# Attention stage of a fused encoder layer: four transpose slots instead of three, a chained minimum for the softmax, and the gate product moved to GpSimd

## The reference, cut to what matters

```python
logits = jnp.einsum('btgrd,btkgd->btgrk', qg, kg).astype(jnp.float32) * (A_HEAD_DIM ** -0.5)
dist = jnp.abs(q_pos[None, :, None] - sel).astype(jnp.float32)
logits = logits - slopes[None, None, :, :, None] * dist[:, :, None, None, :]
logits = jnp.where(valid[:, :, None, None, :], logits, -jnp.inf)
prob = jax.nn.softmax(logits, axis=-1).astype(v.dtype)
out = jnp.einsum('btgrk,btkgd->btgrd', prob, vg)
...
merged = (ga * ((o_a * jax.nn.silu(za)) @ w_a)
```

## Time and profile before

| | us |
|---|---|
| median of 3 runs | 3288.54 (3285.65 to 3290.68) |
| the profiled execution, its own time | 3291.84 |
| its span, first to last instruction | 3290.2 |
| PE busy in it | 2874.0 |
| DVE busy in it | 2378.2 |
| ACT busy in it | 1602.6 |
| POOL busy in it | 1268.2 |

### The profile page before, as it was taken

The page is one execution under the profiler, slowest core; times in us unless marked ns, Lnnn a source line. Parts: engine busy times, 40 slices in busy tenths (PEclk is TensorE's granted clock), DMA queues, the critical chain, the costliest instruction groups (busy, mean ns, idle before and its releaser), DMA issues.

```text
span 3290.2 us, 43028 instructions
## 1 busy us (share of the span) xinstructions
PE 2874.0 (87%) x14677; PEld 2576.1 (78%) x14677; DVE 2378.2 (72%) x4343; ACT 1602.6 (49%) x2638; POOL 1268.2 (39%) x875
## 2 busy tenths in 40 slices
PE   6999998999999989889551778888886999599998
PEld 6999998999999989889430555666666899488886
DVE  7478855839999999998437777787776555455564
ACT  4474787777776766764012555565562000211111
POOL 1100677777787858655222221111002332111120
PEclk9999999999999999999775999999998999799999
DMA  4434223333332323222663222112004555311220
GB/s 153 126 127 149 73 97 105 114 97 112 104 107 92 108 74 103 86 73 95 210 156 111 52 56 48 40 32 52 22 15 166 170 162 181 133 63 62 78 67 33
DMA packets 286182, 321.04 MB, mean 98 GB/s; under 512 B 37025, under 2 KB 258977, under 8 KB 282413
## 3 DMA queue, kind: packets, MB, share of 16 engines
q1 hardware_dynamic: 149037, 176.64, 18.1%
q10 hardware_dynamic: 135648, 137.80, 12.7%
q0 software_dynamic: 1312, 4.26, 0.4%
HBM read 194.46 MB, written 123.48 MB: 97 GB/s over the span
## 4 chain that ended last, share of the span: by engine, by line
PE 46%; DVE 36%; issue 6%; ACT 6%; DMA 4%; POOL 2%; ACTq 1%; SPq 0%; DVEq 0%; POOLq 0%
PE psum L1182 14%; PE psum L2064 12%; DVE s_high L427 10%; PE psum L1939 8%; DVE a_l L1770 4%; DVE a_ptlo L1789 3%; PE psum L1673 2%; PE psum L1709 2%; ACT s_ajunk L410 2%; DVE s_cand L429 2%; ACT v_product L820 1%; DVE s_g L428 1%; PE psum L1162 1%; DVE s_high L459 1%; PE psum L1161 1%
## 5 line engine op out<-in xcount | busy, mean ns | idle before, releaser
L1182 PE MATMUL psum<-hT_hi,j_whi 128*128 128x416 f32 x2440 | 868.0, 356 | 39.0 <-ACT j_out L1055 30.1
L1182 PE MATMUL psum<-hT_hi,j_wlo 128*128 128x416 f32 x2440 | 859.9, 352 | 0.0
L1182 PE MATMUL psum<-hT_lo,j_whi 128*128 128x416 f32 x2440 | 858.9, 352 | 0.0
L834 POOL TENSOR_TENSOR v_y<-v_y,v_product 128x422 f32<-128x422 f32 x580 | 718.5, 1276 | 252.1 <-ACT v_product L820 251.8
L1182 PEld LDWEIGHTS psum<-hT_hi,j_whi 128*128 128x128 f32 x2440 | 461.2, 189 | 56.8 <-ACT j_out L1055 35.2
L1182 PEld LDWEIGHTS psum<-hT_lo,j_whi 128*128 128x128 f32 x2440 | 462.4, 189 | 11.4
L1182 PEld LDWEIGHTS psum<-hT_hi,j_wlo 128*128 128x128 f32 x2440 | 461.3, 189 | 5.8
L427 DVE TENSOR_SCALAR_CACHE_REDUCE s_high<-s_key,s_cand 128x1024 int16<-128x1024 f32 (+4 forms) x240 | 393.0, 1637 | 8.4
L820 ACT ACTIVATE v_product<-v_x,v_taps 128x422 f32<-128x422 f32 x580 | 340.0, 641 | 75.0 <-POOL v_y L834 35.1
L1789 DVE TENSOR_TENSOR a_ptlo<-psum,a_pthi 128x512 fp32r<-128x512 f32 x338 | 228.3, 684 | 56.5 <-ACT a_pthi L1745 55.7
L1738 ACT ACTIVATE a_l<-a_l,a_nbias 128x512 f32<-128x512 f32 (+4 forms) x136 | 184.2, 1354 | 166.7 <-DVE a_nbias L1779 165.3
(11 more groups left out here) (286 smaller groups left out, 5430.2 us busy)
## 6 DMA issues: line engine op xcount, KB each, us to landing
T_dram<-j_out ACTq DMA_DIRECT2D x305, 208.0 KB, 1.9
j_w<-in_w_in ACTq DMA_DIRECT2D x59, 512.0 KB, 4.2
m_gate<-T_dram SPq DMA_DIRECT2D x60, 416.0 KB, 3.5
m_oraw<-B_dram SPq DMA_DIRECT2D x15, 832.0 KB, 6.6
SC_dram<-i_acc SPq DMA_DIRECT2D x40, 256.0 KB, 2.0
M_dram<-m_merged ACTq DMA_DIRECT2D x5, 1664.0 KB, 10.4
n_x<-in_x_prompt SPq DMA_DIRECT2D x16, 512.0 KB, 4.9
a_q<-T_dram SPq DMA_DIRECT2D x32, 256.0 KB, 6.6
```

The costliest lines, as they stand in the source:

```text
L834: pool.tensor_tensor(y[n % 2][:], y[n % 2][:], product[n % RING][:], ALU.add).then_inc(added, 1)
L1182: last = pe.matmul(bank, w[p][:, k, :], h[:, k, t0:t0 + SPAN], start=(k == 0 and q == 0), stop=(k == KD - 1 and q == 2))
```

## The change

It does the following.

1. The ring of transposed weights has a fourth slot, PSUM bank 7, which held the spread reciprocals. These now pass through a slot of the ring as well (`share`, after the weighing of the fourth-last tile), and ACT copies them to SBUF (`shared`, into `factor`).
2. `turn` of tile x + 4 stands behind `weigh` of tile x on PE. Tiles 2 and 3 of a group are turned when the group starts.
3. DVE makes the low part of tile x + 2 at step x (at x = 0 those of tiles 0, 1 and 2), ahead of the score units of the step.
4. The query is scaled by a negative factor, and the distance is added, so that a minimum takes the place of the maximum. Each piece starts from the minimum of the piece before it (`lows`), for which it waits. L1778 and L1779 of before are gone, and the exponential takes the last minimum as its bias, with scale -1.
5. A head's exponential is due four key tiles after its last unit, not two, and behind `shared` in the last step. `finish` stands at x = 1 instead of x = 0.
6. GpSimd multiplies the factor by the gate (`gate`) and the sum of the halves by the factor (`end`); DVE keeps only the addition of the halves. The store moves from GpSimd's queue to SP's, behind the load of the tile after next, and the distances are loaded as soon as the exponentials of two tiles before are done. GpSimd's split of the next query tile stands first in a tile, ahead of the `end` of the group before.
7. Loops with registers are written out.

```diff
-    QK, PT, PO, PB = 2, (2, 3, 4), (5, 6), 7
+    QK, PT, PO = 2, (2, 3, 4, 7), (5, 6)
...
-            if x == 0 and before:
+            if x == 1 and before:
                 e.finish(before)
             for h, at_x in heads:
-                if at_x + 2 <= x:
+                if at_x + RING <= x:
                     e.head(scored, h)
...
+    def sync(sp):
+            if m:
+                sp.wait_ge(exp_done, HEADS * (t - 1))
+            sp.dma_start(nd[p][:, 0:keys], c.ND_dram[t, :, 0:keys]).then_inc(nd_full[p], 16)
...
+        for t in range(TILES):
+            load(t)
+            if t >= 2:
+                store(t - 2)
...
+        def gate(group):
+            u, nu, _ = group.shares
+            pool.wait_ge(pt_free[u], nu + 1)
+            pool.wait_ge(za_full[group.p], group.m * 16 + 16)
+            pool.tensor_tensor(factor[group.g][:], factor[group.g][:], of_group(za, group), ALU.mult).then_inc(factor_made, 1)
+            pool.wait_ge(factor_made, group.n + 1)
+
+        def end(group):
+            o = of_group(oa, group)
+            pool.wait_ge(po_read[group.g], group.t + 1)
+            pool.tensor_tensor(o, o, factor[group.g][:], ALU.mult).then_inc(o_done[group.p], 1)
...
+        for group in groups:
+            if group.g == 0 and 1 <= group.t < TILES - 1:
+                split(group.t + 1)
+            if group.n:
+                end(groups[group.n - 1])
+            gate(group)
...
+        def share(group):
+            u, nu, n = group.shares
+            pe.wait_ge(rs_ready, group.n + 1)
+            pe.wait_ge(pt_free[u], nu)
+            for r, h in enumerate(group.heads):
+                last = pe.matmul(c.psum[:, PT[u], r * P:(r + 1) * P], rs[:, h:h + 1].to_broadcast([P, P]), c.ident[:],
+                                 start=True, stop=True)
...
+        def weigh(group, x, following):
+            pe.wait_ge(pt_free[u], nu + 1)
...
+            if x + RING < tiles:
+                turn(group, x + RING)
+            if x + RING == tiles:
+                share(group)
+            if x + 2 >= tiles and following:
+                turn(following, x + 2 - tiles)
...
+        def shared(group):
+            u, nu, n = group.shares
+            act.wait_ge(pt_full, n + 1)
+            if group.t:
+                act.wait_ge(o_done[1 - group.p], KVH * ((group.t + 1) // 2) - (KVH - 1 - group.g))
+            act.activation(factor[group.g][:], c.psum[0:HD, PT[u], :], ACT.Copy).then_inc(pt_free[u], 1)
...
-            vec.tensor_tensor_reduce(out=L[h][:, a:a + w], in0=c.psum[:, b, 0:w], in1=nd[p][:, a:a + w],
-                                     scale=2.0 ** -(h + 1), scalar=LOWEST, op0=ALU.subtract, op1=ALU.max,
-                                     accum_out=peaks[:, h, s:s + 1]).then_inc(qk_read[b], 1)
...
+            if s:
+                _, _, _, _, previous, uses, _ = group.units[(h - 4 * group.g) * len(pieces(group.keys)) + s - 1]
+                vec.wait_ge(qk_read[previous], uses + 1)
             vec.wait_ge(qk_full, n + 1)
             vec.sem_inc(mark, 1)
+            vec.tensor_tensor_reduce(out=L[h][:, a:a + w], in0=c.psum[:, b, 0:w], in1=nd[group.p][:, a:a + w],
+                                     scale=2.0 ** -(h + 1), scalar=lows[:, h, s - 1:s] if s else HIGHEST, op0=ALU.add, op1=ALU.min,
+                                     accum_out=lows[:, h, s:s + 1]).then_inc(qk_read[b], 1)
...
+        def turned(group, x):
+
+            for ahead in range(3) if x == 0 else (x + 2,):
+                if ahead < len(group.tiles):
+                    low(group, ahead)
```

More of the change, by code:

```diff
@@ L1566, in together @@
+    def together(e, group, scored, before):
+        units, tiles = scored.units if scored else [], group.tiles if group else []
+        if group:
+            e.start(group, before is None)
         issued, heads = 0, []
-        for x in range(max(1, len(keys))):
-            if weighed:
-                e.turned(weighed, keys, x)
-            if x == 0 and before:
+        for x in range(max(1, len(tiles))):
+            if group:
+                e.turned(group, x)
+            if x == 1 and before:
@@ L1571, in together @@
                 e.finish(before)
             for h, at_x in heads:
-                if at_x + 2 <= x:
+                if at_x + RING <= x:
                     e.head(scored, h)
-            heads = [(h, at_x) for h, at_x in heads if at_x + 2 > x]
-            for unit in units[issued:-(-len(units) * 4 * (x + 1) // (3 * len(keys))) if weighed else None]:
+            heads = [(h, at_x) for h, at_x in heads if at_x + RING > x]
+            for unit in units[issued:-(-len(units) * 4 * (x + 1) // (3 * len(tiles))) if group else None]:
@@ L1805, in vector @@
-        own = 2 * TILES + HEADS * (TILES - sum(len(pieces(keys)) == 1 for _, keys in CLASSES) * 4)
-        group_order(Actions(start=start, turned=turned, unit=unit, finish=finish), lambda n: steps.turns(n, own))
+            vec.tensor_tensor_reduce(out=L[h][:, a:a + w], in0=c.psum[:, b, 0:w], in1=nd[group.p][:, a:a + w],
+                                     scale=2.0 ** -(h + 1), scalar=lows[:, h, s - 1:s] if s else HIGHEST, op0=ALU.add, op1=ALU.min,
+                                     accum_out=lows[:, h, s:s + 1]).then_inc(qk_read[b], 1)
```

298 lines of the change are left out of this document (128 added, 170 removed).

## The result

The changed kernel takes 3215.26 us in the median of 4 runs (3212.24 to 3219.06), beside 3287.10 us of the kernel before on the same chip (4 runs, 3282.69 to 3290.68). The ratio is 0.9783, with a 95% interval of 0.9766 to 0.9800: 71.8 us less, where the prediction had 76 less and 3212.5. The profiled execution took 3219.06 us, its span is 3217.2.

A forecast was written before the change was run, and what follows sets the result against it. It took a PE-DVE loop through low parts and scores to bound this stage. Periods, group starts and ends summed to 87 us, less 11 for missed margins: 3291.84 - 76 = 3215.8 profiled, hence 3212.5 median; range 3188 to 3256.

The forecast's parts named there:

- The loop opens: Steady periods of three key tiles: low parts two steps old end PE-DVE waits of 0.82 us, 59 us over 72 periods.
- The period: 4.55 us set by PE: Three key tiles with four score units: PE's work sets 4.55 us, against 5.37 before; DVE's floor is 4.35.
- the 11 us for missed margins: Allowance in the periods for an exponential's late copy passed on to PE: middle of 0 to 22 us.
- Start and end of a group: Group starts and ends, charted: groups take 8.8 us with 512 keys and 25.9 with 2048; 28 us gained.
- The sum by classes: Eight groups each of 512, 1024, 1536 and 2048 keys save 1.4, 2.0, 3.2 and 3.6 us a group.
- Later exponentials cost 2 us a group's end: At each group's end PE waits about 2 us for the later exponentials; included in the sums.
- DVE loses two operations a group, GpSimd's are hidden: DVE sheds two operations of 0.72 us a group; GpSimd gains two of 1.2 us that nobody waits for.
- The last group: Nine tiles weighed without scores, then the final product: about 12.7 us against 16.2, 3.5 less.
- GpSimd bounding the short tiles: Rival: GpSimd operations at twice their rows need 22 us against 17.6 in short tiles; about 3235 us, chance 0.05.
- the period staying at 5.37: Rival: two score banks still tie PE to DVE, only 28 us gained; about 3262 us, chance 0.09.
- Ends give nothing: Rival: PE's wait for the last exponential grows 0.8 us in 34 groups, cancelling 28 us; 3251 us, chance 0.19.
- The chained minimum: Slower rival: each of 208 chained scores on DVE costs c more, using up 76 us at c = 0.43; chance 0.04.

The follow-up runs named there:

- the best order: Changed kernel with the low part between the two score units and the last exponentials ahead of the factor's copy: 3165.59 us; with the chain also taken out, 3164.64 us.

## Why the prediction was right, and where it was off

- **The loop opens.** Right. PE's wait for low parts is gone, and putting the low part back in its own step brings 35 to 41 us and the wait back. Taking away the slot, with the transposes' lead and the due time that go with it, costs 54 to 62, which the text, that spoke of one open loop, left unsplit. The steady period fell from 5.37 to 4.72, not to 4.55: over 72 periods 47 us, where the text had 59.
- **The period: 4.55 us set by PE.** Off. It is 4.72, set by DVE. The term of the sum that was mis-sized is the chained score. I gave it nothing for the scalar and 0.11 us for waiting on its direct predecessor, from two dependent `TENSOR_TENSOR` operations. It costs 0.06 us with each chained score (0.67 from start to start against 0.61), and the directly chained one starts 0.30 later than an independent one: 0.91 us. The experiments without the chain show the other half: the period is 4.54 with the order of the change and with the best order. The bound from above (0.72 for each chained score) held for the score behind a low part and not for the directly chained one, which lay over the 0.8 that the text had named as a sign of being wrong. 72 x 0.17 = 12 us, which is what the 11 us for missed margins came to, though these were meant for ACT's copies and not for DVE: the allowance fitting was luck.
- **Start and end of a group.** Right for 512 keys (8.79 for 8.8), and for the end of long groups within 0.14 us. Of the 0.84 us that a 2048-key group takes too long, four periods of 0.17 would be 0.68, by estimate; on PE the excess shows in the first three, most of it in the second (0.89). With 512 keys two groups of eight took 9.86 and the first 9.63: in the one at 1833.82 the granted clock fell to 0.83 over the group, in the one before it was 1.00, and 12 transposes took 2.77 us (1.47 at full clock, at 2314.50). The two together are 2.1 us.
- **The sum by classes.** Predicted savings 11.2, 16, 25.6 and 28.8 us; measured 7.1, 13.1, 21.2 and 22.2. Together 63.6 of 81.6. Of the 18.0 that are missing, 12 are the chain and 2 the clock; the remaining 4 I did not follow. The 12 stand on 72 x 0.17 and on the experiment without the chain (11.8 in the stage).
- **Later exponentials cost 2 us a group's end.** PE waits 1.6 us a group for the exponential, a little less than that. Moving the last one ahead of the share's copy, one part of it, gives back 13 (medians) to 22 us (stage); the whole price of the later due time has no run of its own, since with the old due time the kernel is 3.8% slower than the kernel before. That the later exponentials could be a condition of the rest was not seen.
- **DVE loses two operations a group, GpSimd's are hidden.** Right in sign: GpSimd needs 1.27 us for each (predicted 1.2), and PE nowhere waits for a query. The worth of the edit was left inside the group charts; taken back alone, it costs as much as the whole gain (76 us), 11 of it by a collision whose ground, two inputs in SBUF, the prediction names only as something that DVE no longer has. The Trainium skill's rule on GpSimd's speed (GPSIMD Engine Reference, 4.1, Engine selection) agrees with the rows for the operation, 1.27 us against 0.68. It is no price for the kernel: DVE is the busy engine at the start of these groups, and 1.27 us on an idle one beats 0.68 on it.
- **The last group.** 14.6 us from its reciprocal to the end of the product (2406.24 to 2420.87), before 16.2 to the store's issue, predicted 12.7. The clock over its first 4.0 us was 0.71, where the same stretch of before had 1.00, and its 12 transposes took 2.50 us.
- **The rivals.** GpSimd bounding the short tiles, and the period staying at 5.37, are both refuted by the rows above. "Ends give nothing" too: PE waits 1.6 us a group for the exponential, as charted, and the ends take what the chart says. The time of "period unchanged" was added up wrongly (3288.5 less 28 is 3260.5 and not 3262), which changes nothing. The chained minimum was the right thing to fear; its c is 0.06 with each chained score and 0.30 more with one a period, under the 0.43 that would have used up the gain.
- **What came from outside.** The total lay nearer than its parts, and that is luck. The stage gave 65.7 of 76 us; 7.3 of the difference of the two profiled spans come from stages that did not change.

## What to carry to other kernels

Take an order of work as a loop through the engines, and for each step ask what the engine's queue holds in front of it: a part made two steps early helped here only with the later exponentials, so that nothing in front of its inputs waited for fresh work of the same engine, and by the waits also only with its slot filled. Price an operation that takes the result of the one before it by a row of the same kind, or give it a wide bound: here independent, scalar-fed and directly chained scores start 0.61, 0.67 and 0.91 us apart. And look for operations that stand in a row at the head of a group and could stand between others: spreading three low parts brought another 34 us.

## What the runs showed of the hardware

- A DVE score with a minimum over its elements takes 680 ns with a constant start value and 744 ns with one read per partition, and one that starts from its direct predecessor's result begins 0.30 us later than an independent one. The predecessor's result is read out by a row of its own (`DVE_READ_ACCUMULATOR2_ANT`, 81 ns in the mean), and the next operation starts 0.30 after that row begins.
- DVE products with two inputs in SBUF ran for up to 2.65 us instead of 0.68 beside GpSimd operations on SBUF, and never over 0.684 us when these were cut to an eighth, nor over 0.686 in the kernel before, whose split came behind them.
- TensorE's granted clock fell from 1.00 to 0.52 (its lower level, 1.2 GHz, for nearly all of the 3 us shown) in a group whose start PE had reached after idling 1.83 us for an exponential:

```profile
1835.00:1838.00 3.00, 3.00 (x15) 2.87 (x14) 1.38 (x2) 1.90 (x5) 0.00 (x0) 0.52 0.99 221
```

This is a window of the changed kernel, with PE busy throughout (us and count for each engine, then clock, DMA share and GB/s). The group at 1852.49 had an idle time of 1.84 us at its start and kept the full clock, so the waits at the group ends are a possible cause and not a shown one. In the whole stage the clock fell to its lower level five times in the changed kernel and twice in the kernel before.
